# Down products two groups behind, eighty exchanged groups, reordered tails and a first unit in quarters

## What is computed

```python
def swiglu(h, w_gate, w_up, w_down):       # 1024 -> 2816 -> 1024
    return (jax.nn.silu(h @ w_gate) * (h @ w_up)) @ w_down

x = x + 0.5 * swiglu(rmsnorm(x, ffn1_norm), ffn1_wg, ffn1_wu, ffn1_wd)
h = rmsnorm(x, mix_norm)
proj = h @ w_in
# block 1: neighbourhood attention (8 heads) and a gated linear attention (4 heads);
# block 2: forgetting attention, dilated attention and a gated recurrence
x = x + jnp.concatenate([...], axis=-1) @ w_out
x = x + 0.5 * swiglu(rmsnorm(x, ffn2_norm), ffn2_wg, ffn2_wu, ffn2_wd)
```

## Time and profile before

| what | us |
| --- | --- |
| median of three runs | 2010.35 (2009.53 to 2012.16) |
| time of the profiled execution | 2007.96 |
| its span, first to last instruction | 2006.2 |
| TensorE busy | 1983.8 (99%) |
| VectorE busy | 1374.9 (69%) |
| ScalarE busy | 1067.5 (53%) |

### The profile page before, as it was taken

One profiled execution on the slowest core, in us unless ns is written; L12 is line 12 of the kernel. 1 busy time (PEld: TensorE's weight loads), 2 busy tenths in 40 slices (PEclk: granted clock), 3 DMA queues, 4 the chain that ended last, 5 costly groups with the idle time before them and its releaser, 6 DMA issues.

```text
span 2006.2 us, 26785 instructions
## 1 busy us (share of the span) xinstructions
PE 1983.8 (99%) x10888; PEld 1663.8 (83%) x10888; DVE 1374.9 (69%) x1688; ACT 1067.5 (53%) x1357; POOL 55.6 (3%) x73
## 2 busy tenths in 40 slices
PE   8999999999999999999999999999999999999998
PEld 7888887888888887888888898888888889888887
DVE  6666976666666696766666669766666666976665
ACT  5545676444544567544554466654455445665444
POOL 3200004000000000000000000000000000000000
PEclk9999999999999999999999999999999999999999
DMA  9765437666566543666566644256656664425662
GB/s 321 249 222 188 162 113 211 228 221 228 193 232 225 177 150 105 220 225 229 195 217 230 227 156 169 107 203 221 227 193 221 227 230 159 168 106 210 221 221 83
DMA packets 145995, 395.62 MB, mean 197 GB/s; under 512 B 81808, under 2 KB 100496, under 8 KB 103504
## 3 DMA queue, kind: packets, MB, share of 16 engines
q1 hardware_dynamic: 142832, 387.49, 55.4%
q0 software_dynamic: 2608, 6.07, 1.4%
q10 hardware_dynamic: 432, 0.35, 0.1%
HBM read 374.21 MB, written 19.66 MB: 196 GB/s over the span
## 4 chain that ended last, share of the span: by engine, by line
PE 87%; DVE 7%; ACT 3%; DVEq 1%; DMA 1%; issue 1%; ACTq 0%; SPq 0%
PE bank L421 83%; DVE w_lo L1219 2%; PE bank L466 1%; PE bank L589 1%; ACT w_hi L821 1%; PE bank L673 1%; DVE arena L1347 1%; PE bank L657 1%; PE bank L635 1%; DMA spill<-scratch 0%; DVE arena L1434 0%; PE bank L603 0%; PE bank L532 0%; DMA x<-xt 0%; DVEq L1435 0%
## 5 line engine op out<-in xcount | busy, mean ns | idle before, releaser
L1219 DVE TENSOR_TENSOR w_lo<-raw,w_hi 128x2048 fp32r<-128x2048 f32 x330 | 757.6, 2297 | 379.5 <-ACT w_hi L821 378.9
L821 ACT ACTIVATE w_hi<-raw 128x2048 fp32r<-128x2048 f32 x330 | 629.7, 1910 | 246.1 <-PE bank L421 242.9
L421 PE MATMUL bank<-w_hi,h_hi 128*128 128x512 f32 x1536 | 602.5, 392 | 1.3 <-DVE arena L1511 0.8
L421 PE MATMUL bank<-w_hi,h_lo 128*128 128x512 f32 x1536 | 598.3, 390 | 0.0
L421 PE MATMUL bank<-w_lo,h_hi 128*128 128x512 f32 x1536 | 598.1, 389 | 0.0
L421 PEld LDWEIGHTS bank<-w_hi,h_hi 128*128 128x128 f32 x1536 | 288.6, 188 | 64.5 <-issue 2.7
L421 PEld LDWEIGHTS bank<-w_hi,h_lo 128*128 128x128 f32 x1536 | 288.5, 188 | 60.5
L421 PEld LDWEIGHTS bank<-w_lo,h_hi 128*128 128x128 f32 x1536 | 288.7, 188 | 58.8
L421 PE MATMUL bank<-w_hi,act_hi 128*128 128x512 f32 x832 | 327.8, 394 | 2.9 <-DVE act_lo L1568 2.1
L421 PE MATMUL bank<-w_hi,act_lo 128*128 128x512 f32 x832 | 324.2, 390 | 0.0
L421 PE MATMUL bank<-w_lo,act_hi 128*128 128x512 f32 x832 | 324.0, 389 | 0.0
(11 more groups left out here) (213 smaller groups left out, 1403.4 us busy)
## 6 DMA issues: line engine op xcount, KB each, us to landing
raw<-stream SPq DMA_DIRECT2D x331, 1024.0 KB, 4.9
spill<-scratch SPq DMA_DIRECT2D x71, 256.0 KB, 3.7
scratch<-spill SPq DMA_DIRECT2D x71, 256.0 KB, 2.6
arena<-rpb POOLq DMA_DIRECT2D x32, 96.0 KB, 9.5
x<-xt SPq DMA_DIRECT2D x4, 256.0 KB, 5.5
raw<-stream SPq DMA_DIRECT2D x2, 512.0 KB, 5.9
arena<-final_gain POOLq DMA_DIRECT2D x2, 512.0 KB, 4.4
out<-x SPq DMA_DIRECT2D x3, 256.0 KB, 2.5
```

The source lines that it names most:

```text
L421: last = mm(o, a, r, start=start and n == 0, stop=stop and n == len(pairs) - 1)
L821: fn(w_hi[u % SLOTS][:, :], raw[u % RAW][:, :], ACT.Copy).then_inc(hi_done, 1)
L1219: tt(w_lo[u % SLOTS][:, :], raw[u % RAW][:, :], w_hi[u % SLOTS][:, :].bitcast(F32), ALU.subtract).then_inc(lo_done, 1)
```

## The change

- The order of the units becomes f0 b0 f1 b1 f2 b2 d0 f3 b3 d1 ... f10 b10 d8 d9 d10. `turn_act(10)` stands between d8 and d9. Stream order, `ffn_use`, and the splits of ScalarE and VectorE follow.
- Gate and up use `PD` for group 0, `PB` for odd groups and `PX` for even ones (`gate_banks`); `PT` is bank 0.
- All groups but the last of each FFN are exchanged: 80, and 8 are turned.
- Before `act_high(g - 1)` both engines now split f of the next group, and for g < 3 also the unit behind it.
- The first half of the first unit is split in two quarters, and x pieces 2 and 3 are transposed behind the first twelve matmuls.
- Block one's tail: ScalarE's split of the third output unit moves ahead of the last head's copy; VectorE's low half of r = 2 moves ahead of the fourth gain.
- Block two's tail: `recurrence_turns` moves from behind product (0, 3) of unit r = 0 to behind (1, 0), that is by three matmuls.

```diff
-EXCHANGED = [at for at in ALL_GROUPS if 0 < at[3] < GROUPS - 1 and at != (0, 0, 0, 1)]
+EXCHANGED = [at for at in ALL_GROUPS if at[3] < GROUPS - 1]
...
-        XB, PT = bank[0:2] + bank[6:8], bank[6]
+        XB, PT = bank[0:2] + bank[6:8], bank[0]
...
             if kind == "down":
-                off = 3 * g + 4 if g < GROUPS - 1 else FFN_UNITS - 1
+                off = 3 * g + 6 if g < GROUPS - 2 else FFN_UNITS - GROUPS + g
             else:
-                off = (3 * g - 1 if g else 0) + (kind == "back")
+                off = (3 * g - 2 if g else 0) + (g == 1) + (kind == "back")
...
+        def gate_banks(g):
+
+            return PD if g == 0 else PB if g % 2 else PX
...
-                for i in range(4):
+                for i in range(2):
                     wait_x(pe, v, i)
-                    turn(None, x, i // 2, i % 2)
+                    turn(None, x, 0, i)
...
-                    if g >= 2:
-                        pe.wait_ge(a_ready, 2 * ffn_no(b, L, j, g))
+                    if g >= 3:
+                        pe.wait_ge(a_ready, 2 * ffn_no(b, L, j, g - 1))
                     for kk in range(4):
-                        if u == 0 and kk % 2 == 0:
-                            pe.wait_ge((half_lo, lo_done)[kk // 2], 1)
+                        if u == 0 and kk < 3:
+                            pe.wait_ge((first_lo, half_lo, lo_done)[kk], 1)
...
+                        if u == 0 and kk == 1:
+                            for i in range(2, 4):
+                                wait_x(pe, v, i)
+                                turn(nn, x, 1, i - 2)
...
-                front(PD, 0)
-                back(PD, 0)
-                for g in range(1, GROUPS):
-                    front(PB, g)
-                    if (b, L, j, g - 1) in TURNED:
-                        turn_act(g - 1)
-                    back(PB, g)
-                    down(g - 1, {(0, 3): lambda: turn_act(GROUPS - 1)} if g == GROUPS - 1 else {})
+                for g in range(GROUPS):
+                    front(gate_banks(g), g)
+                    back(gate_banks(g), g)
+                    if g >= 2:
+                        down(g - 2)
+                turn_act(GROUPS - 1)
+                down(GROUPS - 2)
...
                         if b == 1 and r == 0:
-                            between[0, 3] = lambda: recurrence_turns(b, L)
+                            between[1, 0] = lambda: recurrence_turns(b, L)
...
+                    if g >= 2:
+                        act.wait_ge(used, use_of("down", g - 2) + 1)
                     fn(act_hi[g % 2][:, :, :].rearrange("p a b -> p (a b)"), src, ACT.Copy).then_inc(ahi_ready, 1)
...
                     turned_hi(b, L, 2 * j, [0])
+                    act.wait_ge(raw_half, 16)
+                    for q in range(2):
+                        cols = slice(q * UNIT // 4, (q + 1) * UNIT // 4)
+                        fn(w_hi[0][:, cols], raw[0][:, cols], ACT.Copy).then_inc((first_hi, half_hi)[q], 1)
+                    turned_hi(b, L, 2 * j, [1])
                     half_high(0, 1)
-                    turned_hi(b, L, 2 * j, [1, 2, 3])
+                    turned_hi(b, L, 2 * j, [2, 3])
...
                 for g in range(1, GROUPS):
+                    split(use_of("front", g) + SLOTS)
+                    if g < 3:
+                        split(use_of("back", g) + SLOTS)
                     act_high(g - 1)
-                    split(use_of("front", g) + SLOTS)
                     gates(g)
-                    split(use_of("back", g) + SLOTS)
+                    if g >= 3:
+                        split(use_of("back", g) + SLOTS)
...
-                    split(use_of("down", g - 1) + SLOTS)
+                    if 2 <= g < GROUPS - 1:
+                        split(use_of("down", g - 2) + SLOTS)
+                    if g == GROUPS - 1:
+                        split(use_of("down", g - 1) + SLOTS)
...
+                    if b == 0 and r == 0:
+                        split(mix_use(b, L, nunits + 2))
                     if turned is not None:
                         copy_head(turned)
...
                 for g in range(1, GROUPS):
+                    split(use_of("front", g) + SLOTS)
+                    if g < 3:
+                        split(use_of("back", g) + SLOTS)
                     if (b, L, j, g - 1) in EXCHANGED:
                         act_turn(g - 1)
                     act_low(g - 1)
-                    split(use_of("front", g) + SLOTS)
                     gated(g)
+                    if g >= 3:
+                        split(use_of("back", g) + SLOTS)
                     if g == GROUPS - 1:
-                        split(use_of("back", g) + SLOTS)
                         act_low(g)
-                    else:
-                        split(use_of("back", g) + SLOTS)
+                        split(use_of("down", g - 2) + SLOTS)
...
                         dve.wait_ge(nrs, L + 1)
-                        for k in range(2):
-                            for c in range(2 * k, 2 * k + 2):
-                                ins = stt(h[:, c, :], h[:, c, :], gain(b, L, "ogain", c), rs[:, :], ALU.mult, ALU.mult)
-                            ins.then_inc(mix_ready, 1)
-                        mixed_lo(b, L, 2)
+                        for c in range(4):
+                            if c == 3:
+                                mixed_lo(b, L, 2)
+                            ins = stt(h[:, c, :], h[:, c, :], gain(b, L, "ogain", c), rs[:, :], ALU.mult, ALU.mult)
+                            if c % 2:
+                                ins.then_inc(mix_ready, 1)
```

More of the change, by code:

```diff
@@ L185, in build @@
         table_loaded, raw_half = sem("table_loaded"), sem("raw_half")
+        first_hi, first_lo = sem("first_hi"), sem("first_lo")
         y_ready, y_gained, y_scaled = sem("y_ready"), sem("y_gained"), sem("y_scaled")
@@ L823, in half_high @@
             def half_high(u, half):
-                if (u, half) == (0, 0):
-                    act.wait_ge(raw_half, 16)
-                else:
-                    act.wait_ge(raw_ready[u], 16)
+                act.wait_ge(raw_ready[u], 16)
                 cols = slice(half * UNIT // 2, (half + 1) * UNIT // 2)
@@ L884, in gates @@
                             act.wait_ge(used, use_of("back", g) + 1)
-                        src = (PD if g == 0 else PB)[t][:, 0:256]
+                        src = gate_banks(g)[t][:, 0:256]
                         fn(gate_s[:, t, :], src, ACT.Sigmoid, scale=rms[:, t:t + 1]).then_inc(sig_done, 1)
@@ L1151, in mixing @@
                         split_mixed(3)
-                    if b == 0 and r == 0:
-                        split(mix_use(b, L, nunits + 2))
-                    elif late and not (b == 0 and i == nunits - 1):
+                    if late and not (b == 0 and i in (nunits - 1, nunits)):
                         split(mix_use(b, L, i + 3))
@@ L1177, in _ @@
             act.wait_ge(const_set, 2)
-            half_high(0, 0)
             act.wait_ge(params_loaded, 16)
@@ L1261, in gated @@
                     no = ffn_no(b, L, j, g)
-                    banks = PD if g == 0 else PB
+                    banks = gate_banks(g)
                     for t in range(2):
@@ L1301, in ffn @@
                     turned_lo(b, L, 2 * j, [0])
+                    for q in range(2):
+                        cols = slice(q * UNIT // 4, (q + 1) * UNIT // 4)
+                        dve.wait_ge((first_hi, half_hi)[q], 1)
+                        tt(w_lo[0][:, cols], raw[0][:, cols], w_hi[0][:, cols].bitcast(F32), ALU.subtract).then_inc((first_lo, half_lo)[q], 1)
+                    turned_lo(b, L, 2 * j, [1])
                     half_low(0, 1)
-                    turned_lo(b, L, 2 * j, [1, 2, 3])
+                    turned_lo(b, L, 2 * j, [2, 3])
                     for half in range(2):
@@ L1333, in ffn @@
                         tt(code_lo[:, :], w, code_hi[:, :].bitcast(F32), ALU.subtract).then_inc(code_split, 1)
-                    if g < GROUPS - 1:
-                        split(use_of("down", g - 1) + SLOTS)
+                    if 2 <= g < GROUPS - 1:
+                        split(use_of("down", g - 2) + SLOTS)
             def halves(ap, m):
@@ L1782, in _ @@
             tt(diag[:, :], ident[:, 0:64], ident[:, 64:P], ALU.add)
-            half_low(0, 0)
             dve.wait_ge(params_loaded, 16)
@@ L1909, in down @@
                         out.append(rows.reshape(4, 2, 32, D).transpose(0, 2, 1, 3).reshape(P, UNIT))
-                gate_up(0)
-                for n in range(1, GROUPS):
+                for n in range(GROUPS):
                     gate_up(n)
-                    down(n - 1)
+                    if n >= 2:
+                        down(n - 2)
+                down(GROUPS - 2)
                 down(GROUPS - 1)
```

## The result

The changed kernel takes 2015.37 us (median of 10 runs, 2013.84 to 2017.21), the kernel before, run beside it, 2009.88 (10 runs, 2006.93 to 2012.16): a ratio of 1.003, 95% interval 1.0022 to 1.0039, so it is 5.5 us slower (the interval says 4.4 to 7.8). The forecast was 2011.7 us and no change, with a range from 2003 to 2017. The profiled execution took 2015.1 us, its span is 2013.3 us: 7.1 us more than in the earlier trace rows. The profiles differ by more than the medians because the profiled execution of the kernel before, 2007.96 us, lies 1.9 us under that kernel's median of the ten runs.

The account below looks back on a forecast made before the run. TensorE, busy 1983.8 of 2006.2 us, was taken as the bound. First FFN's loss 7.8, less turned groups 3.4 and tails 3.0, gave +1.4 on 2007.96; with 2.4 for the median, 2011.7 us, own range 2009 to 2014.4, wide range 2003 to 2017.

Parts of the forecast that it names:

- rival 2: First FFN: POOL's loads hold up the first exchange's return, decisive from T0 = 44.1; 2015.9 us at 45.6; chance 0.22.
- No change: Whole kernel: time stays within 0.2%, 4.0 us, of the kernel before; chance 0.50.
- Turned groups, -3.4: Seven later FFNs: each group no longer turned saves TensorE 0.48 us, 3.4 us in all, with the exchange hidden.
- Tails, -3.0: Mixing tails: 0.78 us won twice in block one, 0.7 twice in block two; 3.0 taken, bounds 0 to 3.6.
- Quarters, +0.9: First unit: quartering starts b0 at 18.0 instead of 17.1, a 0.9 us loss; bounds gain 1.9, loss 1.3.
- First exchange, T0 = 41.5: First FFN: return issued at 36.1 lands at 41.5 beside `rpb` loads at half rate; bounds 38.8 and 45.6.
- T0: First FFN: the moment the first exchange's return lands, forecast 41.5 us, from which the later chain is counted.
- f3's unit, 55.1: First FFN: weight unit for group 3's front ready at 55.1, TensorE there at 50.7, a wait of 4.4 us.
- d1's unit, 69.8: First FFN: weight unit for group 1's down product ready at 69.8, TensorE there at 66.0, a wait of 3.7 us.
- Rival 1: First FFN: exchanges of groups 0 and 1 hide; sum -6.8, 2003.5 us; chance 0.28.

Follow-up runs that it names:

- nine_turned: Changed kernel with the old set of turned groups (group 0 of every FFN and group 1 of the first), 71 exchanged; 2007.25 us, ratio 0.999.
- two_turned: Changed kernel with groups 0 and 1 of the first FFN turned by TensorE again, 78 groups exchanged; 2004.28 us, ratio 0.9976.
- tails_only: Kernel before with only the three edits of the mixing tails; 2005.84 us, ratio 0.9983.
- kept_busy: Changed kernel with 14 idle matmuls ahead of f3 and 30 ahead of d1 in the first FFN; 2014.29 us, ratio 1.0027.
- tables_later: Changed kernel with the table steps of VectorE and ScalarE in the first FFN two groups later; 2011.88 us, ratio 1.0012.
- rpb_late: Changed kernel with POOL's sixteen first-layer `rpb` loads issued only after fourteen weight units are split; 2007.47 us, ratio 0.9994.
- one_turned: two_turned, but with group 1 of the first FFN exchanged, so group 0 alone is turned there; 2013.10 us, ratio 1.0017.
- combined: two_turned with the first unit in halves again and the turn of group 1 behind b2 instead of f2; 2004.53 us, ratio 0.9976.

## Why the prediction was right, and where it was off

The mechanism held: the loss sits in the first FFN's two exchanges, the later FFNs hide theirs, and tails and turned groups give some of it back. The size was off, by 3.7 us in the medians: 2015.37 us lies 1.0 us above the forecast's own range, 2009 to 2014.4, and inside the wide one only because that one had room for rival 2. In the profiles the sum came out as 13.6 - 6.5 = +7.1 us where 7.8 - 3.4 - 3.0 = +1.4 was forecast. "No change" had the chance of 0.50, "slower" 0.22; the measured 0.3% is slower by the bound given.

- **Turned groups, -3.4.** Right: 3.0 us in nine_turned against two_turned, 0.42 us a group for a forecast 0.48. 32 transposes are left, and no other FFN waits for an exchange; the 0.6 us at the start of block two is a wait of another kind.
- **Tails, -3.0.** Right, and nearly the upper bound of 3.6: 3.4 us in tails_only, and of the two waits 0.2 us are left in the changed kernel. In the changed timeline of VectorE the subtraction of the weight unit starts here:

```profile
317.15 2.28 DVE L1237 TENSOR_TENSOR w_lo<-raw,w_hi 128x2048 fp32r<-128x2048 f32 x1
```

  The old order would have it at 304.70 + 13.6 = 318.3. That is 1.2 us earlier, where 0.95 was forecast.
- **Quarters, +0.9.** b0's first matmul starts at 18.69, 0.7 us later than forecast (the first product itself started at 9.49, not at 8.9). The loss of 1.5 us against 17.16 is more than the bound of 1.3. TensorE's share of it does not reach the end, as f3 waits in any case. What the edit is worth depends on the rest: +3.4 us on the kernel before and, from kernels of different sets and so less sure, +1.4 with two turned groups and -1.8 with the exchanges.
- **First exchange, T0 = 41.5.** Right in the end, partly by luck: the return was issued at 35.27, 0.8 us earlier than the 36.1 forecast, and took 6.9 us beside the `rpb` loads where half the rate, my price, gave 5.4. The two misses nearly cancel; transposes started at 42.18. The spill's price depends on the execution as well: with the same edit it took 4.3 us here, 5.6 in kept_busy and 5.8 in tables_later. The rule of the Trainium skill (DMA: Bandwidth & Descriptors, Queues, rings and completion order), by which the landing was put near 40, was 2 us too early; that queues take turns agrees with the rows of 51.5:58.3, where both moved.
- **f3's unit, 55.1.** Right: 55.2, and a wait of 3.6 us for 4.4.
- **d1's unit, 69.8.** This is the term that was mis-sized: it was ready at 74.3. The step was "its own exchange lands by about 57". It was never worked out: I priced the contention with loads and `rpb` for the first exchange and took the second as free. The transposes started at 61.05 instead of 57.4, 3.7 us late, and the low half of the activation took 0.8 us more; together 4.5. rpb_late (7.9 us gained) and one_turned (still 2013.1 with the first exchange gone) show that the second exchange decides. Its price could have been read before: in the trace of the kernel before the spill of group 2 took 61.96 - 52.55 = 9.4 us, and the `rpb` loads were over at 58.78. An estimate from the first: issued at 46.5, the spill ends at 55.9 and the transposes start near 58.7, 1.3 us later than assumed. From the second, if the spill ends with the `rpb` loads as it did: near 61.6, where 61.05 was measured.
- **The clock.** Not in the sum at all: 1.7 us behind d1. 7.8 + 4.5 + 1.7 is 14.0 (the prediction's own terms give 8.2 for its 8.1, a matter of rounding). d1 started 0.1 us behind its unit. The old order lost some 0.5 us more around its own early waits than I had counted: b3 starts at 61.65 there and f4, two units on, at 73.32 instead of 72.5, of which 0.3 was in the sum. That leaves 13.6.

**Rivals.** Rival 1 (the exchanges hide) was wrong, with two waits of 3.6 and 5.4 us. Rival 2's time, 2015.9, is nearest to the result, but its mechanism did not occur: T0 was 42.1, under its bound of 44.1. The hold-up by POOL's loads was real and hit the second exchange's spill hardest (11.0 us, 2.6 without them); the first one's return took 6.9 us beside them and 3.8 in rpb_late.

The kernel before has a spread of its own of which the prediction knew nothing: 2006.9 to 2012.2 us. tails_only's long execution shows a cause that can do this, the same kind of spill (13.2 us) and a wait of 4.3 us in the old order; that it is behind the whole spread is only argued.

What stays open: how much of the second spill's delay belongs to loads 9 and 10 and how much to POOL. Of the 11.0 us, 4.3 pass behind the loads and 6.8 beside `rpb`. rpb_late removes both at once: without the `rpb` loads, loads 9 and 10 land in 7.1 us instead of up to 14.6, before the spill is issued. Behind weight loads and with little of `rpb` left, a spill took 9.4 us in the kernel before; but those loads had themselves run beside `rpb`.

## What to carry to other kernels

Price each of a chain of transfers with what lies on its queue and beside it at its own moment; a price worked out for the first one does not hold for the next, which may be queued behind the loads that the first released. Take its price from the slowest transfer of its kind in the trace, not from an undisturbed one, unless its neighbours are known. A longer lag hides a transfer in steady state, but not in the first groups, where there are no earlier groups to work on: keep the path without DMA there (turned groups 0 and 1) and take the exchange elsewhere, which here gave 2002.9 us. When a wait of some microseconds on TensorE is forecast, add the slow matmuls behind it, but only where nothing else is late there.

## What the hardware showed that was not expected

- The same spill of 256 KB in 1,040 packets took 2.6 us alone, 4.3 to 7.7 us as the first spill, behind a load, and 11.0 to 15.9 us (six kernels, kept_busy the longest) behind loads of its queue and beside POOL's loads, with whose end it ended.
- The length of a TensorE wait alone does not say what the clock does. After 3.6 us it was at 1.2 GHz for 12 matmuls, after 5.4 us for 8; after 1.6 us (two_turned) and after 3.3 us ahead of the idle matmuls (kept_busy) it stayed at 2.4 GHz. In combined, 6 matmuls at the full clock followed a wait of 1.9 us before 8 slow ones came, and in rpb_late 5 followed a wait of 3.4 us before 7 slow ones.
- With idle matmuls behind 3.3 us of the second wait the clock was at 2.4 GHz when d1 came, which was worth 1.6 us of its time; the medians differ by 1.1 us.
